# A convolutional decoder layer on 8 cores: LayerNorm steps of group A issued in pairs, with other PSUM banks

## The chip, the cores and the metric

The kernel runs on the 8 cores of one Trainium2 chip. Each core works on one prompt sequence (2064 positions: 16 meta tokens and 2048 tokens) and on 16 of the 128 sample sequences (8 positions each); the cores exchange nothing. The metric is the device time in microseconds of the slowest core. The runs of the kernel before took 1062.82, 1060.1 and 1065.99 us; the median is 1062.82.

## What is computed

One layer of a decoder with two head groups, then a convolutional FFN. The part around the change is group A:

```
h = rmsnorm(x)
a_val, a_gate, b_gate, c_gate, b_in = split(h @ w_in)
u  = a_val * sigmoid(a_gate)
ua = causal_depthwise_conv(u, width 31) + bias
ya = silu(layernorm_per_head(ua) * g + b) * beta_a        # 64 channels a head
yb = beta_b * b_gate * causal_depthwise_conv(c_gate * b_in, width 3)
x  = x + concat(ya, yb) @ w_out
h  = rmsnorm(x); up = causal_depthwise_conv(h @ w_up, width 3)
x  = x + (silu(up_gate) * up_val) @ w_down;  y = rmsnorm(x)
```

The updated convolution states are outputs as well. Weights and activations come as 32-bit floats; the large matmuls work in bf16.

## The kernel before, in words

The positions of a core are worked through in three **passes** (`PASSES`): 656 prompt positions, 768, and 640 with the 128 sample positions behind them. Channels lie on the partitions, positions on the columns. Within a pass the prompt columns are cut in two halves (`ntiles`: 328, 384 or 320 columns), and in the last pass the 128 sample columns are a third part. A pass runs through these stages: row norm and transposes; group A's input projection with the gate; group B whole; **group A's convolution and LayerNorm**; the output projection in tiles of 128 positions (`p3_tile`, L829 to L859), with the second row norm; the FFN (up projection, width-3 convolution, down projection).

All work is given to a small list (`Prog.add`): each operation names an engine, the buffers that it reads and those that it writes. Each engine executes its operations in the order of the list and waits on semaphores for the operations that it depends on. So the order of the calls is the order of every engine, and a wait holds up all that stands behind it on that engine. A PSUM bank is one buffer (`ps0` to `ps7`): a new matmul group in a bank waits until the bank's last reader is done.

Group A's stage has `nj` **jobs**: one for each of 4 channel blocks in each column part, 8 jobs in the first two passes and 12 in the last (the last four with 128 columns). Each job goes through six functions (L761 to L827):

- `s0` (L761): the width-31 convolution as 31 matmuls with diagonal weights (L773), into bank 2 or 3.
- `s0a` (L777): ScalarE adds the bias and copies to SBUF (L781, Identity).
- `s1` (L785): a matmul subtracts the mean of each head (L790), into bank 4 or 5; ScalarE squares it (L793).
- `s2` (L796): a matmul forms the variance (L800), into bank 6 or 7; ScalarE takes the square root (L804).
- `s3` (L807): VectorE takes the reciprocal (L813) and multiplies it with the centred value, which it reads from s1's bank (L815).
- `s4` (L818): ScalarE applies Silu with scale and bias (L821); VectorE multiplies by beta and writes the column block of `mixT` (L824).

The loop over `it` (L861) issues, in this order, s0 of job `it`, s3 of `it-3`, s4 of `it-4`, s2 of `it-2`, s1 of `it-1` and s0a of `it`: a software pipeline written out by hand. Sqrt and Silu need different function tables of ScalarE, so an `ACT_TABLE_LOAD` stands ahead of each change between them; Square, Identity and Copy run without one. Results of three sqrts can be held (`RB`), squares too (`t_dsq`), and two of `t_ua` and `t_yn`.

Once all convolutions are issued (`it >= nj`), each turn of the loop also issues one output tile as soon as the jobs of its columns have had s4. A tile is 4 groups of 8 matmuls (L846), each followed by VectorE's add into the residual (L850); the banks go round 0 to 3. Behind a tile stand the row norm of the tile before (`norm_stats`: ScalarE L480, L483; VectorE L485, L487) and the transposes of the tile three before (`norm_trans`, L498, L501, banks 4 and 5). In the last pass the conv states are transposed into banks 0 and 1 and stored between the loop and the remaining tiles (L874 to L892).

Of the kernel before, what the change touches and what calls it, by code (L numbers as in the profile page):

```python
# [169 lines left out]
def build(debug=False):  # L170
# [145 lines left out]
    def w_next():  # L316
        n = wcur["n"]
        wcur["n"] += 1
        assert n < wstate["issued"]
        return n, ring[n % NSLOT], f"w{n % NSLOT}"  # L320
# [170 lines left out]
    def norm_trans(j, nt, col, bsel, b):  # L491
        h = hn[bsel]
        pv = psb_bf(b).rearrange("p (k n) -> p k n", k=8)

        def f_T(e):
            ins = None
            for k in range(8):
                ins = e.transpose(out=pv[:, k, 0:nt], in_=h[0:nt, k * 128:(k + 1) * 128], identity=ident_b[0:nt, 0:nt])  # L498
            return ins
        P.add("pe", f_T, reads=[f"hn{bsel}", "ident_b"], writes=[f"ps{b}"])  # L500
        P.add("act", lambda e: e.activation(out=hT[:, :, col:col + nt], in_=pv[:, :, 0:nt], func=AF.Copy),  # L501
              reads=[f"ps{b}"], writes=[f"hT{j}"])
# [33 lines left out]
    for pi, (p0, sp, samp) in enumerate(PASSES):  # L536
# [11 lines left out]
        def ntiles_of(col, nt):  # L548
            return [t for (t, n0, nw, kind) in ntiles if n0 < col + nt and n0 + nw > col]
# [106 lines left out]
        for cp in range(2):  # L656
            for cc in range(2):
                c = cp * 2 + cc
# [98 lines left out]
        jobs = [(c, t, n0, nw, kind) for (t, n0, nw, kind) in ntiles for c in range(4)]  # L757
        RB = [(t_sig[0], "sig0"), (t_sig[1], "sig1"), (t_cg[0], "cg0")]
        nj = len(jobs)

        def s0(i):  # L761
            c, t, n0, nw, kind = jobs[i]
            b = 2 + i % 2
            rk = [f"dg{c}", f"u{c}_{t}", (f"u{c}_{t - 1}" if (kind == "p" and t > 0) else (f"uh{c}" if kind == "p" else f"ush{c}"))]

            def f_conv(e):
                ins = None
                for k in range(31):
                    if kind == "p":
                        rhs = ubuf_p[:, c, n0 + k:n0 + k + nw]  # L770
                    else:
                        rhs = ubuf_s[:, c, :, k:k + 8]
                    ins = e.matmul(ps[:, b, 0:nw], lhsT=dg[:, c * 31 + k, :], rhs=rhs, start=(k == 0), stop=(k == 30))  # L773
                return ins
            P.add("pe", f_conv, reads=rk + [LM], writes=[f"ps{b}"])

        def s0a(i):  # L777
            c, t, n0, nw, kind = jobs[i]
            b = 2 + i % 2
            sl = i % 2  # L780
            P.add("act", lambda e: e.activation(out=t_ua[sl][:, 0:nw], in_=ps[:, b, 0:nw], func=AF.Identity,  # L781
                                                bias=prm[:, PBC + c:PBC + c + 1]),
                  reads=[f"ps{b}", "prm", LM], writes=[f"ua{sl}"])

        def s1(i):  # L785
            c, t, n0, nw, kind = jobs[i]
            b = 4 + i % 2
            sl = i % 2
            s3_ = i % 3
            P.add("pe", lambda e: e.matmul(ps[:, b, 0:nw], lhsT=Cmat, rhs=t_ua[sl][:, 0:nw],  # L790
                                           start=True, stop=True),
                  reads=["Cmat", f"ua{sl}"], writes=[f"ps{b}"])
            P.add("act", lambda e: e.activation(out=t_dsq[s3_][:, 0:nw], in_=ps[:, b, 0:nw], func=AF.Square),  # L793
                  reads=[f"ps{b}", LM], writes=[f"dsq{s3_}"])

        def s2(i):  # L796
            c, t, n0, nw, kind = jobs[i]
            b = 6 + i % 2
            s3_ = i % 3
            P.add("pe", lambda e: e.matmul(ps[:, b, 0:nw], lhsT=Bd_r, rhs=t_dsq[s3_][:, 0:nw],  # L800
                                           start=True, stop=True),
                  reads=["Bd_r", f"dsq{s3_}"], writes=[f"ps{b}"])
            rb, rk_ = RB[s3_]
            P.add("act", lambda e: e.activation(out=rb[:, 0:nw], in_=ps[:, b, 0:nw], func=AF.Sqrt, bias=eps_ap),  # L804
                  reads=[f"ps{b}", "eps", LM], writes=[rk_])

        def s3(i):  # L807
            c, t, n0, nw, kind = jobs[i]
            bD = 4 + i % 2
            sl = i % 2  # L810
            s3_ = i % 3
            rb, rk_ = RB[s3_]
            P.add("dve", lambda e: e.reciprocal(out=rb[:, 0:nw], in_=rb[:, 0:nw]),  # L813
                  reads=[rk_], writes=[rk_])
            P.add("dve", lambda e: e.tensor_tensor(out=t_yn[sl][:, 0:nw], in0=ps[:, bD, 0:nw], in1=rb[:, 0:nw], op=ALU.mult),  # L815
                  reads=[f"ps{bD}", rk_, LM], writes=[f"yn{sl}"])

        def s4(i):  # L818
            c, t, n0, nw, kind = jobs[i]
            sl = i % 2  # L820
            P.add("act", lambda e: e.activation(out=t_yn[sl][:, 0:nw], in_=t_yn[sl][:, 0:nw], func=AF.Silu,  # L821
                                                scale=prm[:, PGG + c:PGG + c + 1], bias=prm[:, PGB + c:PGB + c + 1]),
                  reads=[f"yn{sl}", "prm"], writes=[f"yn{sl}"])
            P.add("dve", lambda e: e.tensor_scalar(out=mixT[:, c, n0:n0 + nw], in0=t_yn[sl][:, 0:nw],  # L824
                                                   scalar1=prm[:, PBA + c:PBA + c + 1], scalar2=None, op0=ALU.mult),
                  reads=[f"yn{sl}", "prm", LM], writes=[f"mx{c}_{t}"])

        p3 = {"idx": 0, "jo": 0, "wn4": None}
        KORD = (4, 5, 6, 7, 0, 1, 2, 3)  # L829

        def p3_tile():
            if p3["wn4"] is None:
                p3["wn4"] = [w_next() for _ in range(4)]
            wn4 = p3["wn4"]
            idx = p3["idx"]
            p3["idx"] += 1
            (j, col, nt, kind) = ttiles[idx]
            mk = [f"mx{c}_{t}" for c in range(8) for t in ntiles_of(col, nt)]
            for q in range(4):
                b = p3["jo"] % 4  # L840
                p3["jo"] += 1

                def f_mo(e, r=wn4[q][1], b=b):
                    ins = None
                    for i_, k in enumerate(KORD):
                        ins = e.matmul(ps[0:nt, b, 0:256], lhsT=mixT[:, k, col:col + nt], rhs=r[:, k, :],  # L846
                                       start=(i_ == 0), stop=(i_ == 7))
                    return ins
                P.add("pe", f_mo, reads=[wn4[q][2]] + mk + [LM], writes=[f"ps{b}"])
                P.add("dve", lambda e, b=b, q=q: e.tensor_tensor(  # L850
                    out=xres[0:nt, j, 256 * q:256 * (q + 1)], in0=ps[0:nt, b, 0:256], in1=xres[0:nt, j, 256 * q:256 * (q + 1)],
                    op=ALU.add),
                    reads=[f"ps{b}", f"xr{j}"], writes=[f"xr{j}"])
            if idx >= 3:
                (j2, col2, nt2, kind2) = ttiles[idx - 3]
                norm_trans(j2, nt2, col2, par(j2), 4 + par(j2))
            if idx >= 1:
                (j2, col2, nt2, kind2) = ttiles[idx - 1]
                norm_stats(j2, nt2, 1, par(j2))  # L859

        for it in range(nj + 4):  # L861
            for (fn, lag) in ((s0, 0), (s3, 3), (s4, 4), (s2, 2), (s1, 1), (s0a, 0)):
                if 0 <= it - lag < nj:
                    fn(it - lag)
            if it >= nj and p3["idx"] < len(ttiles):
                (j_, col_, nt_, kind_) = ttiles[p3["idx"]]
                if all(it >= 4 * t_ + 7 for t_ in ntiles_of(col_, nt_)):
                    p3_tile()
# [28 lines left out]
        while p3["idx"] < len(ttiles):  # L897
            p3_tile()
# [110 lines left out]
        jo = 0  # L1009
# [128 lines left out]
def _get_nc():  # L1138
    if "nc" not in _NC_CACHE:
        _NC_CACHE["nc"] = build()  # L1140
    return _NC_CACHE["nc"]
# [46 lines left out]
```

How the kernel before makes its waits and increments, by code:

```python
    def emit_engine(self, eng, e, semobj, final_waits=False):  # L123
        waited = {}
        for op in self.ops:
            if op.eng != eng:
                continue
            for d in op.deps:
                if waited.get(d.sem, 0) < d.val:
                    e.wait_ge(semobj[d.sem], d.val)
                    waited[d.sem] = d.val
            ins = op.fn(e)
            if op.sem is not None:
                ins.then_inc(semobj[op.sem], 16 if op.dma is not None else 1)
        if final_waits:
            for name, v in self.final_dma.items():
                k = ("dma", name)
                if waited.get(k, 0) < v:
                    e.wait_ge(semobj[k], v)
```

## Time and profile before

| | before |
|---|---|
| median of 3 runs | 1062.82 us (1060.1 to 1065.99) |
| the profiled execution | 1053.46 us |
| its span, on core 3, the slowest | 1051.9 us |
| spans of the 8 cores | 1029.4 to 1051.9 us |
| mean granted TensorE clock of the cores | 0.945 to 0.957 |
| group A's stage, passes 1, 2, 3 (first conv to first output tile) | 109.4 to 152.6, 412.7 to 461.8, 750.9 to 809.1 us |

The profile is one execution on one core, with times in us from the start of the span. A row of the groups by line names the source line, the engine, the operation, output and input, the count, the total and the mean duration, and the idle time of the engine ahead of it. The chain of waits follows the work that ended last back to its releasers and lists its pieces by time: start, duration, what. A timeline lists an engine's instructions: start, duration, engine, line, operation; in square brackets the time for which the engine had been idle and who released it. PE is TensorE, ACT ScalarE, DVE VectorE.

### The profile page before, as it was taken

The page shows a single profiled execution, that of the slowest core. Times are in us where ns is not written, and L with a number is a line of the kernel's source. Part 1 is how long each engine was busy: PE and PEld are TensorE (multiplying, and loading weights), DVE is VectorE, ACT ScalarE, POOL GpSimd, SP SyncE. Part 2 cuts the span into 40 slices and gives each one's busy share as a digit, 9 for nine tenths or more (in the row PEclk, how much of TensorE's full clock was granted, in tenths as well). Part 3 has the DMA queues.
Part 4 walks back from the last instruction along what each step waited for, and adds up shares of the span by engine and source line. Part 5 has one row for each costly group of instructions (what it writes and reads, how often), then busy time and mean ns, then how long its engine had stood idle before and what let it go on. Part 6 is the DMA issues. An engine that isn't in the chain of part 4 may idle for free.

```text
span 1051.9 us, 21154 instructions; the slowest of 8 cores (1029.4 to 1051.9 us)
## 1 busy us (share of the span) xinstructions
PE 913.3 (87%) x6993; PEld 668.0 (64%) x6993; DVE 654.4 (62%) x933; ACT 594.4 (57%) x1069; POOL 295.8 (28%) x464
## 2 busy tenths in 40 slices
PE   1769987799979899976799998979997679999997
PEld 0436655577758666555466667857766567777886
DVE  2227456499972577366399993458455548999614
ACT  3313385688871433584688872243378558888432
POOL 3003100287721213001177750023200024444200
PEclk9979988899989999988899999989997889999999
DMA  9999500889858799000878774799900067877522
GB/s 198 182 119 159 68 1 21 103 107 116 108 76 107 169 196 155 12 1 6 111 94 111 92 97 57 160 170 113 121 1 1 14 85 85 102 96 90 69 55 121
DMA packets 154569, 98.55 MB, mean 94 GB/s; under 512 B 3592, under 2 KB 148264, under 8 KB 154446
## 3 DMA queue, kind: packets, MB, share of 16 engines
q0 software_dynamic: 146688, 73.93, 56.8%
q1 hardware_dynamic: 7774, 23.27, 6.9%
q8 instruction: 58, 0.95, 0.4%
q14 instruction: 49, 0.40, 0.1%
HBM read 161.04 MB, written 10.79 MB: 163 GB/s over the span
## 4 chain that ended last, share of the span: by engine, by line
PE 67%; DMA 9%; DVE 8%; ACT 6%; issue 6%; SPq 2%; DVEq 0%; POOL 0%; ACTq 0%; POOLq 0%
PE ps L507 39%; PE ps L1018 11%; PE ps L773 9%; PE ps L846 6%; DMA arena<-sf 4%; DVE arena L955 3%; DVE arena L813 2%; SPq L349 2%; DMA yp<-arena 2%; ACT arena L480 1%; PE ps L498 1%; ACT arena L934 1%; DVE arena L487 1%; DMA ncfs<-arena 1%; DMA arena<-xs 1%
## 5 line engine op out<-in xcount | busy, mean ns | idle before, releaser
L507 PE MATMUL ps<-arena 128*128 128x328 bf16 (+3 forms) x3584 | 499.5, 302 | 18.2 <-ACT arena L620 10.6
L507 PEld LDWEIGHTS ps<-arena 128*128 128x128 bf16 x3584 | 334.9, 100 | 177.9 <-issue 25.6
L955 DVE SCALAR_TENSOR_TENSOR arena<-arena 128x656 f32<-128x656 f32 (+2 forms) x264 | 255.6, 989 | 42.0 <-ACT arena L951 19.8
L1018 PE MATMUL ps<-arena 128*128 128x256 bf16 x1496 | 166.9, 274 | 2.0 <-DVE arena L977 1.7
L1018 PEld LDWEIGHTS ps<-arena 128*128 128x128 bf16 x1496 | 146.7, 98 | 20.3 <-issue 2.7
L934 ACT ACTIVATE arena<-ps 128x328 f32<-128x328 f32 (+2 forms) x264 | 116.9, 454 | 40.4 <-PE ps L507 30.3
L303 POOL DMA_DIRECT2D arena<-w_up x66 | 57.7, 877 | 287.1 <-PE ps L846 245.6
L773 PE MATMUL ps<-arena 128*128 128x328 bf16 (+3 forms) x868 | 123.2, 301 | 0.0
L951 ACT ACTIVATE arena<-arena 128x656 f32<-128x656 f32 (+2 forms) x132 | 114.8, 902 | 7.4 <-DVE arena L925 7.4
L773 PEld LDWEIGHTS ps<-arena 128*128 128x128 bf16 x868 | 80.6, 99 | 36.7 <-issue 0.3
L813 DVE RECIPROCAL arena<-arena 128x328 f32<-128x328 f32 (+3 forms) x28 | 59.0, 2108 | 68.5 <-ACT arena L804 68.5
L846 PE MATMUL ps<-arena 128*128 128x256 bf16 (+1 forms) x576 | 79.7, 307 | 22.0 <-DVE arena L824 12.7
L846 PEld LDWEIGHTS ps<-arena 128*128 128x128 bf16 (+1 forms) x576 | 62.0, 110 | 38.1 <-issue 24.5
L1023 DVE TENSOR_TENSOR arena<-ps,arena 128x256 f32<-128x256 f32 x68 | 28.0, 423 | 89.5 <-PE ps L1018 89.3
L922 POOL COPY arena<-arena 128x2 f32<-128x2 f32 x132 | 73.1, 572 | 15.3 <-POOL arena L960 7.6
L501 ACT ACTIVATE arena<-ps 128x1024 bf16<-128x1024 bf16 (+1 forms) x36 | 35.2, 979 | 69.0 <-PE ps L498 69.0
L498 PE MATMUL ps<-arena 128*128 128x128 bf16 (+1 forms) x288 | 25.5, 243 | 52.3 <-DVE arena L487 27.0
L960 POOL COPY arena<-arena 128x2 f32<-128x2 f32 x88 | 52.1, 592 | 47.4 <-ACT arena L934 42.1
L977 DVE TENSOR_TENSOR arena<-arena 128x656 bf16<-128x656 f32 (+2 forms) x66 | 57.8, 875 | 11.1 <-ACT arena L975 6.6
L975 ACT ACTIVATE arena<-arena 128x656 f32<-128x656 f32 (+2 forms) x66 | 54.2, 822 | 18.4 <-DVE arena L955 18.1
L588 DVE TENSOR_TENSOR arena<-arena 128x1024 bf16<-128x1024 f32 (+1 forms) x48 | 56.8, 1183 | 0.0
L498 PEld LDWEIGHTS ps<-arena 128*128 128x128 bf16 (+1 forms) x288 | 20.7, 110 | 56.3 <-issue 55.6
(85 smaller groups left out, 717.5 us busy)
## 6 DMA issues: line engine op xcount, KB each, us to landing
arena<-w_up POOLq DMA_DIRECT2D x66, 512.0 KB, 8.5
arena<-w_in POOLq DMA_DIRECT2D x30, 512.0 KB, 23.3
arena<-w_down POOLq DMA_DIRECT2D x24, 512.0 KB, 7.1
arena<-xp SPq DMA_DIRECT2D x16, 512.0 KB, 10.7
yp<-arena SPq DMA_DIRECT2D x16, 512.0 KB
arena<-w_out POOLq DMA_DIRECT2D x12, 512.0 KB, 15.6
arena<-w_down POOLq DMA_DIRECT2D x12, 384.0 KB, 7.0
arena<-g SPq DMA_DIRECT2D x3, 512.0 KB, 11.7
```

The lines of the kernel that those rows point to most:

```text
L303: P.add("pool", lambda e, dst=dst, src=src: e.dma_start(out=dst, in_=src), writes=[f"w{slot}"], dma=f"ws{slot}")
L507: ins = e.matmul(ps[:, b, 0:nw], lhsT=r[:, k, off:off + 128], rhs=hT[:, k, n0:n0 + nw], start=(k == 0), stop=(k == 7))
L588: P.add("dve", lambda e: e.tensor_tensor(out=dg[:, c * 31 + k0:c * 31 + k1, :], in0=ident_f.unsqueeze(1).broadcast_to([128, nk, 128]), in1 ...
L773: ins = e.matmul(ps[:, b, 0:nw], lhsT=dg[:, c * 31 + k, :], rhs=rhs, start=(k == 0), stop=(k == 30))
L813: P.add("dve", lambda e: e.reciprocal(out=rb[:, 0:nw], in_=rb[:, 0:nw]), reads=[rk_], writes=[rk_])
L846: ins = e.matmul(ps[0:nt, b, 0:256], lhsT=mixT[:, k, col:col + nt], rhs=r[:, k, :], start=(i_ == 0), stop=(i_ == 7))
L922: P.add("pool", lambda e, rs_=rs_, ci=ci: e.tensor_copy(out=raw[rs_][:, 0:2], in_=hist_f[:, ci, :]), reads=["hist_f", LF], writes=[f"rawh{ ...
L934: P.add("act", lambda e, rs_=rs_, b=b, n0=n0, nw=nw: e.activation(out=raw[rs_][:, 2 + n0:2 + n0 + nw], in_=ps[:, b, 0:nw], func=AF.Copy), ...
L951: P.add("act", lambda e, rs_=rs_, wk=wk, fw=fw: e.activation(out=acc[rs_][:, 0:fw], in_=raw[rs_][:, 0:fw], func=AF.Copy, scale=wk[0]), rea ...
L955: P.add("dve", lambda e, rs_=rs_, wk=wk, k=k, fw=fw: e.scalar_tensor_tensor(out=acc[rs_][:, 0:fw], in0=raw[rs_][:, k:k + fw], scalar=wk[k] ...
L977: P.add("dve", lambda e: e.tensor_tensor(out=actT[:, j, 0:sp], in0=acc[rg_][:, 0:sp], in1=acc[rv_][:, 0:sp], op=ALU.mult), reads=akeys_g + ...
L1018: ins = e.matmul(ps[0:nt, b, 0:256], lhsT=actT[:, k, col:col + nt], rhs=wd3[k // 8][1][:, k % 8, :], start=(k == 0), stop=(k == 21))
```

## The change

The centred value's bank is chosen by a new function `dbank`: bank 1 for all odd jobs, banks 4 and 5 by turns for the even ones. The square root leaves `s2` and becomes a function of its own, `s2a`. s3, s4 and s2a are each issued for two jobs at once: s3 in even turns of the loop, s4 and s2a in odd turns, so that ScalarE's two Silus follow each other and its two Sqrts too. The output tiles use banks 0, 2 and 3 instead of 0 to 3.

```diff
+        def dbank(i):
+            return (4 + (i // 2) % 2) if i % 2 == 0 else 1
+
         def s1(i):
             c, t, n0, nw, kind = jobs[i]
-            b = 4 + i % 2
+            b = dbank(i)
...
             P.add("pe", lambda e: e.matmul(ps[:, b, 0:nw], lhsT=Bd_r, rhs=t_dsq[s3_][:, 0:nw],
                                            start=True, stop=True),
                   reads=["Bd_r", f"dsq{s3_}"], writes=[f"ps{b}"])
+
+        def s2a(i):
+            c, t, n0, nw, kind = jobs[i]
+            b = 6 + i % 2
+            s3_ = i % 3
             rb, rk_ = RB[s3_]
             P.add("act", lambda e: e.activation(out=rb[:, 0:nw], in_=ps[:, b, 0:nw], func=AF.Sqrt, bias=eps_ap),
                   reads=[f"ps{b}", "eps", LM], writes=[rk_])
 
         def s3(i):
             c, t, n0, nw, kind = jobs[i]
-            bD = 4 + i % 2
+            bD = dbank(i)
...
             for q in range(4):
-                b = p3["jo"] % 4
+                b = (0, 2, 3)[p3["jo"] % 3]
                 p3["jo"] += 1
...
+        assert nj % 2 == 0
         for it in range(nj + 4):
-            for (fn, lag) in ((s0, 0), (s3, 3), (s4, 4), (s2, 2), (s1, 1), (s0a, 0)):
-                if 0 <= it - lag < nj:
-                    fn(it - lag)
+            if it < nj:
+                s0(it)
+            if it % 2 == 0:
+                for i_ in (it - 4, it - 3):
+                    if 0 <= i_ < nj:
+                        s3(i_)
+            else:
+                for i_ in (it - 5, it - 4):
+                    if 0 <= i_ < nj:
+                        s4(i_)
+            if 0 <= it - 2 < nj:
+                s2(it - 2)
+            if it % 2 == 1:
+                for i_ in (it - 3, it - 2):
+                    if 0 <= i_ < nj:
+                        s2a(i_)
+            if 0 <= it - 1 < nj:
+                s1(it - 1)
+            if it < nj:
+                s0a(it)
             if it >= nj and p3["idx"] < len(ttiles):
```

## Rows read from the trace of the kernel before

**Rows 1.** The page's first part: busy us, share of the span, instructions.

```profile
PE 913.3 (87%) x6993; PEld 668.0 (64%) x6993; DVE 654.4 (62%) x933; ACT 594.4 (57%) x1069; POOL 295.8 (28%) x464
```

**Rows 2.** Groups by line, the whole span: the two table loads of the stage.

```profile
L821 ACT ACT_TABLE_LOAD x28 | 35.9, 1283 | 3.8 <-DVE arena L815 3.4
...
L804 ACT ACT_TABLE_LOAD x25 | 32.1, 1283 | 29.1 <-PE ps L800 28.8
```

**Rows 3.** Chain of waits, first pass, 105 to 200 us: start, us, what.

```profile
118.21 4.34 PE ps L773 x31
...
133.93 0.54 ACT arena L804
...
134.56 2.21 DVE arena L813
...
136.87 0.51 DVE arena L815
...
137.51 0.39 PE ps L790
137.90 4.34 PE ps L773 x31
...
152.61 5.27 PE ps L846 x32
...
171.74 5.96 PE ps L846 x32
```

**Rows 4.** Timeline of ScalarE, first pass: start, us, instruction, idle before.

```profile
134.36 0.44 ACT L793 ACTIVATE lnbuf<-ps 128x328 fp32r<-128x328 f32 x1
134.68 0.54 ACT L781 ACTIVATE lnbuf<-ps,arena 128x328 fp32r<-128x328 f32 x1
135.24 1.28 ACT L821 ACT_TABLE_LOAD   x1
136.53 0.66 ACT L821 ACTIVATE arena<-arena 128x328 f32<-128x328 f32 x1
137.28 1.28 ACT L804 ACT_TABLE_LOAD   x1
138.57 0.54 ACT L804 ACTIVATE arena<-ps,arena 128x328 f32<-128x328 f32 x1
139.00 0.44 ACT L793 ACTIVATE lnbuf<-ps 128x328 fp32r<-128x328 f32 x1
```

**Rows 5.** Timeline of VectorE, drain of the first pass.

```profile
161.09 0.38 DVE L824 TENSOR_SCALAR arena<-arena 128x328 bf16<-128x328 f32 x1
161.39 2.01 DVE L850 TENSOR_TENSOR arena<-ps,arena 128x256 f32<-128x256 f32 x4
...
164.83 2.18 DVE L813 RECIPROCAL arena<-arena 128x328 f32<-128x328 f32 x1
```

**Rows 6.** Chain of waits, whole span: last conv and two tiles, pass 2.

```profile
450.49 5.07 PE ps L773 x31
...
461.80 5.92 PE ps L846 x32
...
482.46 5.91 PE ps L846 x32
```

**Rows 7.** Chain of waits, last pass, 745 to 860 us.

```profile
797.69 3.33 PE ps L773 x31
...
809.10 6.34 PE ps L846 x32
...
823.17 3.65 PE ps L846 x32
...
831.71 4.38 DMA ncap<-arena
...
836.90 6.17 PE ps L846 x32
```

**Rows 8.** Busy time, tail of last pass: PE, PEld, DVE, ACT, POOL, clock.

```profile
788.00:809.00 21.00, 13.45 (x136) 12.34 (x137) 12.09 (x15) 20.44 (x30) 0.00 (x0) 0.81 0.00 1
```

## The prediction

> **What bounds the kernel now.** I read the page's first part, then the groups by line, then the chain of waits and the timelines of the group-A stage in each of the three passes. TensorE is busy 87% of the span and ScalarE 57% [rows 1]. ScalarE reloads its function table 25 times ahead of the Sqrt of L804 and 28 times ahead of the Silu of L821, 1.283 us each [rows 2]: 53 loads, 68.0 us of ScalarE, which the change wants to halve. What those loads cost must be read from the stage. I call the job's steps conv (L773), ident (L781), C (L790, the mean taken off), square (L793), S (L800, the variance), sqrt (L804), rec and tt (L813, L815), silu (L821), TS (L824).
>
> In the first pass the third conv starts at 118.21 and the seventh at 137.90: four jobs in 19.69 us, 9.85 for a pair [rows 3]. A conv lasts 4.34; with S and C, 0.15 each when nothing holds them, a job needs 4.64 and a pair 9.28. So TensorE loses only 0.57 us per pair here, where C waits for tt (the C at 137.51, released by the tt at 136.87 [rows 3]). One whole turn of ScalarE, from the square at 134.36 to that at 139.00 (0.43 behind the sqrt at 138.57), takes 4.64 us too, of which 2.58 are loads [rows 4]: it just keeps up. Only with the four 128-column jobs of the last pass is ScalarE the bound: busy 20.44 of 21.00 us, with a granted clock of 0.81 [rows 8]. Behind the convs comes the drain: the output projection (L846, "tiles") runs between the last jobs, and its fourth tile (p3 tile 3) waits for the last TS. It starts at 171.74 [rows 3] and 482.46 [rows 6]; VectorE is the bound there, as rec takes 2.21 us [rows 3].
>
> **The change, part by part.** *Table loads.* In the new order the pair's two silus follow each other, and the two sqrts. 28 jobs are 14 pairs: 14 loads for L804 and 14 for L821, 25 fewer, 32 us less ScalarE time, plus a few fewer in front of the Sqrt of the row norm. In the convs this is hidden (TensorE paces); on the path it could give back the 0.57 per pair and most of the last pass's tail.
>
> *The bank of the odd C.* All odd jobs' C outputs now go to bank 1, and the even ones alternate 4 and 5. C of odd job i is issued in iteration i+1; the bank's reader is tt of job i-2, which is now issued in that same iteration, second of a pair, behind two recs. Its sqrt was issued in the iteration before, behind two silus, which themselves stand behind square and ident of the iteration before that. This closes a ring from one odd C to the next. Its length at 328 columns, by starts of successive rows: C end to square 0.10, square 0.32, ident 0.55, load 1.29 [rows 4], two silus 0.55 + 0.68 (the first without a load behind it: 0.66 less the 0.11 by which neighbours overlap, as square at 134.36 and ident at 134.68), load 1.29 [rows 4]; sqrt start to rec start 0.63, rec 2.31, tt 0.43 (0.51 less an overlap), rec 2.31, tt 0.51, release 0.14, C 0.39 [rows 3]. Sum 11.50 us per pair, against 9.28 that TensorE needs and 9.85 now. The saved load is in it: without pairing only one rec stood in the ring, and C alternated between two banks.
>
> When does it bite? New conv 4 starts at 118.21 + 2 x 4.64 = 127.49 and conv 5 at 132.13. C(3) finds its bank free (tt(1) ends near 131.2, conv 4 at 131.8). Then square(3) 132.23, ident(4) 132.55, and 0.55 + 1.29 + 0.55 + 0.68 + 1.29 gives sqrt(2) at 136.91, rec at 137.54, tt(3) end at 137.54 + 5.56 = 143.10, C(5) done and conv 7 started at 143.63; before it is 142.54 (137.90 + 4.64): +1.1. C(7), one ring later, ends at 155.1 and tile 0 starts at about 155.3 against 152.61 [rows 3]: **+2.7 at the end of the convs**. For 384 columns I scale VectorE's and TensorE's durations by columns and add 0.05 to each of ScalarE's: ring 12.6 against 2 x (5.07 + 0.35) = 10.8 [rows 6]. By the same steps conv 7 starts at 451.7 instead of 450.49, and tile 0 at 464.5 instead of 461.80: +2.7. In the last pass (320 columns, then 128) four Cs are caught: conv 7 +1.1, C(7) +2.9, C(9) +5.0 (its ring still holds two 320-column recs, though the convs are short), C(11) +6.2 (its recs have 128 columns): tile 0 at 815.3 instead of 809.10 [rows 7].
>
> *The drain.* Before, VectorE alternates rec, tt, TS of one job and the four adds of a tile. Now rec and tt of the last pair stand together behind tile 1's adds and the row norm of tile 0, and both last TS behind tile 2's adds and the norm of tile 1. Pass 1: tile 0 lasts 5.27 [rows 3], S 0.35, tile 1 3.65, so tile 1's last add ends near 164.95; norm 1.5 (adds from 161.39 to next rec at 164.83, less their 2.0 [rows 5]) 166.5; rec, tt, rec, tt 5.5: 171.9. Tile 2's fourth group now shares a bank with its first (three banks 0, 2, 3 instead of four), whose add waits for this: add and release 0.6, group in the low clock and its latency 1.97, so the last add starts at 174.5; then 0.3, norm 1.5, two TS 0.75 [rows 5], release 0.15: tile 3 starts at 177.2 instead of 171.74: **+5.4**, the 2.7 above within it. Pass 2 by scaling: 487.9 instead of 482.46, +5.4. *Three banks once more:* in tile 4 the fourth group waits for the first's add, which stands behind a norm. This wait already stood at tile 5, but one more group (0.9) now lies behind it. Bounds: 0 (the add comes in time) and 2.1 (a full add chain); I take 0.9, which is one group of tile 1. Passes 1 and 2: **+6.3 each**.
>
> *Last pass.* Tile 3 needs no 128-column job. It starts near 831.3 and, its fourth group waiting for both TS and one add, ends at 835.4; before it ended at 823.17 + 3.65 = 826.8 [rows 7]: +8.6. Then the state outputs: ScalarE waits 4.38 for a DMA, and tile 4 only starts behind it at 836.90, because its first bank is bank 0, into which the transposed state goes [rows 7]. After the change its first two groups have banks 2 and 3 and can run in that wait: two groups at the low clock. Bounds 1.8 (warm groups) and 3.5 (cold, 6.17 for four of which two are quick); I take -3.0. In tile 5 the fourth group waits for an add behind a norm: +2.1. Sum **+7.7**.
>
> Total 6.3 + 6.3 + 7.7 = 20.3 us. Nothing later absorbs it: the stages behind start on the last tile's transposes, and their weights lie in the ring. The sum is made against the profiled execution, 1053.46 us with a span of 1051.9 on core 3; the median of the runs is 1062.82, 0.9% above. I add the sum to the median: **1083 us**, +1.9%. The stage's work is the same on all cores.
>
> **Clock.** In the last pass's tail short waits already bring a conv of 31 matmuls to 3.33 us and the clock to 0.81 [rows 7, 8], and tile 0 takes 5.27 and 6.34 where a warm tile takes 3.65 [rows 3, 7]: 1.2 GHz after waiting, 2.4 GHz later. The waits of the new ring (1 to 2 us each) could do this to convs 7. A conv at half speed costs 4.3 more, but S(5), sqrt(5) and rec(5) behind it come only 1 us later than rec(4) allows, so the ring hides the rest. The Trainium skill ("TensorE: Matmul & The Clock Gate", section "A second HAM failure mode: psum-queue depth-cycling") says that short idles between matmul groups, as the kernel cycles through banks, make the clock swing. The tail's 0.81 agrees, while the full convs, with waits of 0.3 us, keep their 4.34; by that rule the sum would be that of rival 4.
>
> **Rivals.**
> 1. *Faster: the loads were the limit and the bank ring isn't.* Each pair saves 2.57 us of ScalarE. If rec of the pair's first job starts so early that tt(odd) ends before the second conv, that is if the ring is below 9.3, the 0.57 per pair goes (some 2 us over the three passes), ScalarE's bound in the tail falls by half of its 8 loads (5 us), and the bank shift gives 3: about -10, **1053 us**. For it: rows 8. Against: even with C, its release, square and ident left out (1.5), 10.0 us remain in the ring: two loads, two silus, a sqrt, both recs and both tts. Chance 0.07. The Trainium skill ("ScalarE: Activation LUTs", section "Rules for kernel authors") says to group calls by table set and to do all of one before switching, and budgets about 2.7 us for a switch; by that figure 25 loads would be 67 us of ScalarE. The trace has 1.283 us a load, and the trace goes.
> 2. *The ring binds, the drain doesn't get longer* (TS and adds fill gaps I count as lost): 2.7 + 2.7 + 6.2, less 3 for the bank, is +8.6, **1071 us**. Against: VectorE's order is fixed in the program, and its idle time would sit ahead of the last pair. Chance 0.14.
> 3. *Gains and losses meet*: the ring binds by half (say 5 us in all), the tail and the bank give it back: **1063 us**. Chance 0.07.
> 4. *The clock falls in the ring and stays low through the drain*: 1 us at each conv 7, 1 to 2 us in each drain where a second tile runs slow: +5, **1088 us** or some more. Chance 0.14.
>
> **How the numbers follow.** The forecast as worked out has 0.58. The range takes in rivals 2 and 4 and the bounds of the bank terms (-3.5 to +2.1) with the runs' own spread of 3 us either side: 1069 to 1094. About 0.5% is what a measurement of this kernel can tell from no change, 1057.5 to 1068. Slower by more: 0.58 + 0.14 + 0.14 = 0.86; within: 0.07; faster: 0.07.
>
> **What would show it.** Right: loads at L804 and L821 14 each; L790 waits for L815 about 2 us at every second job from C(5) on; conv starts 4.64 apart, then pairs of 11.5; tile 3 about 5.4 us further behind the first conv; L846's idle up by some 10 us, in passes 1 and 2 partly before a fourth group; tile 4 of the last pass starting before L892 ends. Wrong: L790 not waiting for L815 in the middle of the convs, or pairs near 9.3. If sqrt starts well before the conv's end with the ring shorter, the silu spacing is my mistake; if the clock in the convs is below 0.9, rival 4.

## The result and the profile after

The changed kernel took 1085.96 us (median of 9 runs, 1078.39 to 1096.58), the kernel before 1062.09 us (10 runs) beside it. The ratio is **1.028, with a 95% interval of 1.022 to 1.034**: slower by some 23 to 36 us. The profiled execution took 1087.73 us, its slowest core (7) a span of 1086.2. The medians' difference (24 us) and the ratio (about 30 us) don't agree closely, since in some runs the cores of one die or of both have a lower granted clock and take longer, and only the ratio leaves these out (in the experiments below "four cores" are those of the undisturbed die, and four kernels have no ratio for this reason). The profiles spread less: I read three stretches in each pass, on all eight cores, and give the median over the cores.

| stretch, us (passes 1, 2, 3) | before | after | difference |
|---|---|---|---|
| first conv to tile 0 | 43.3, 49.1, 58.1 | 46.0, 51.9, 64.4 | +2.7, +2.8, +6.3 |
| tile 0 to tile 3 | 19.6, 20.6, 13.8 | 22.4, 23.1, 15.6 | +2.8, +2.5, +1.8 |
| tile 3 to the FFN's first matmul | 23.5, 24.1, 28.6 | 28.1, 29.4, 30.8 | +4.6, +5.3, +2.2 |
| sum of the nine (median of the cores' sums) | 280.9 (278.3 to 284.4) | 310.5 (306.8 to 314.0) | **+29.6** |

The sum of the nine agrees with the ratio, so the loss lies in the stage of the change. In pass 3, tiles 2 and 3 often run on without a pause, and there the start of tile 3 is interpolated, here and below. Taken from its first matmul, the changed kernel's last two stretches of pass 3 are 15.9 and 30.6 us instead of 15.6 and 30.8; the sums are not touched by this.

First the part of the page that gives the busy times, then the groups by line with the loads, C's matmul (now L793) and the tiles (now L854):

```profile
PE 928.0 (85%) x6993; PEld 676.2 (62%) x6993; DVE 655.2 (60%) x933; ACT 557.7 (51%) x1041; POOL 297.9 (27%) x464
```

```profile
L854 PE MATMUL ps<-arena 128*128 128x256 bf16 (+1 forms) x576 | 87.6, 324 | 31.4 <-DVE arena L858 25.0 <-DVE arena L832 5.7 <-ACT arena L918 0.7
...
L812 ACT ACT_TABLE_LOAD x14 | 18.0, 1283 | 0.2
L829 ACT ACT_TABLE_LOAD x14 | 18.0, 1283 | 7.1 <-DVE arena L823 6.9
...
L793 PE MATMUL ps<-lnbuf 128*128 128x328 f32 (+3 forms) x28 | 10.7, 384 | 23.5 <-DVE arena L823 23.5
...
L483 ACT ACT_TABLE_LOAD x5 | 6.4, 1283 | 0.4
```

The same two matmul groups before, C's (L790) and the tiles' (L846):

```profile
L846 PE MATMUL ps<-arena 128*128 128x256 bf16 (+1 forms) x576 | 79.7, 307 | 22.0 <-DVE arena L824 12.7 <-DVE arena L850 5.1 <-ACT arena L892 4.3
...
L790 PE MATMUL ps<-lnbuf 128*128 128x328 f32 (+3 forms) x28 | 10.9, 389 | 11.5 <-DVE arena L815 11.5
```

The loads fell as the change says: 14 and 14 instead of 53 [rows 2], and 5 instead of 8 ahead of the norm's Sqrt. ScalarE is busy 557.7 us instead of 594.4 [rows 1], and the kernel is slower: TensorE now stands idle 23.5 us ahead of C, waiting for tt (L823), instead of 11.5, and 31.4 us ahead of the tiles instead of 22.0. Of the latter, the waits for the adds (L858, before L850) rose from 5.1 to 25.0 us.

The chain of waits of pass 1 on core 7 (start, us, what) shows the first ring. The first conv starts at 112.25 here and at 109.40 before:

```profile
134.98 4.34 PE ps L773 x31
...
140.41 2.21 DVE arena L821
...
143.14 2.20 DVE arena L821
...
145.44 0.51 DVE arena L823
...
146.08 0.38 PE ps L793
146.47 4.34 PE ps L773 x31
...
151.90 2.21 DVE arena L821
...
154.62 2.20 DVE arena L821
...
156.92 0.51 DVE arena L823
...
158.18 5.67 PE ps L854 x32
```

Conv 5 starts at 134.98, right behind C(3). Conv 7 starts at 146.47, and tile 0 at 158.18: 11.49 and 11.71 us apart, with two recs ahead of each. [Rows 3] have one rec there and 9.85 us for two convs. ScalarE's timeline of the same turn:

```profile
135.07 0.44 ACT L796 ACTIVATE lnbuf<-ps 128x328 fp32r<-128x328 f32 x1 [3.49 <-PE ps L793]
135.41 0.53 ACT L781 ACTIVATE lnbuf<-ps,arena 128x328 fp32r<-128x328 f32 x1
135.96 1.28 ACT L829 ACT_TABLE_LOAD   x1
137.25 1.21 ACT L829 ACTIVATE arena<-arena 128x328 f32<-128x328 f32 x2
138.48 1.28 ACT L812 ACT_TABLE_LOAD   x1
139.78 0.96 ACT L812 ACTIVATE arena<-ps,arena 128x328 f32<-128x328 f32 x2
```

From the square at 135.07 to the first sqrt at 139.78 pass 4.71 us with one silu more than in [rows 4], and only then can the first rec start, at 140.41.

### The profile page after: what moved, and what is told of

It is laid out like the page before. It is cut to its first block, busy times and chain, and to the rows that moved or that the text cites. A ratio compares the mean times of both kernels' runs of the same rounds, so it can differ in the third digit from the quotient of the medians.

```text
span 1086.2 us, 21098 instructions; the slowest of 8 cores (1060.8 to 1086.2 us)
## 1 busy us (share of the span) xinstructions
PE 928.0 (85%) x6993; PEld 676.2 (62%) x6993; DVE 655.2 (60%) x933; ACT 557.7 (51%) x1041; POOL 297.9 (27%) x464
## 4 chain that ended last, share of the span: by engine, by line
PE 64%; DVE 12%; ACT 7%; DMA 7%; issue 7%; SPq 2%; DVEq 0%; POOL 0%; ACTq 0%; POOLq 0%
PE ps L507 35%; PE ps L1044 12%; PE ps L773 8%; PE ps L854 6%; DVE arena L981 5%; DVE arena L821 4%; DMA arena<-sf 4%; SPq L349 2%; ACT arena L480 2%; ACT arena L977 2%; PE ps L498 1%; DMA yp<-arena 1%; DMA arena<-xs 1%; DVE arena L487 1%; PE ps L793 1%
## 5 line engine op out<-in xcount | busy, mean ns | idle before, releaser
L507 PE MATMUL ps<-arena 128*128 128x328 bf16 (+3 forms) x3584 | 503.0, 304 | 17.8 <-ACT arena L620 9.8
L773 PE MATMUL ps<-arena 128*128 128x328 bf16 (+3 forms) x868 | 126.4, 307 | 0.0
L854 PE MATMUL ps<-arena 128*128 128x256 bf16 (+1 forms) x576 | 87.6, 324 | 31.4 <-DVE arena L858 25.0
L854 PEld LDWEIGHTS ps<-arena 128*128 128x128 bf16 (+1 forms) x576 | 64.8, 115 | 51.6 <-issue 35.3
L948 POOL COPY arena<-arena 128x2 f32<-128x2 f32 x132 | 75.9, 593 | 16.4 <-POOL arena L986 7.6
L986 POOL COPY arena<-arena 128x2 f32<-128x2 f32 x88 | 53.7, 610 | 47.0 <-ACT arena L960 41.1
L1001 ACT ACTIVATE arena<-arena 128x656 f32<-128x656 f32 (+2 forms) x66 | 54.3, 823 | 21.2 <-DVE arena L981 20.7
L858 DVE TENSOR_TENSOR arena<-ps,arena 128x256 f32<-128x256 f32 (+1 forms) x72 | 30.5, 423 | 46.2 <-PE ps L854 43.2
L498 PEld LDWEIGHTS ps<-arena 128*128 128x128 bf16 (+1 forms) x288 | 22.4, 116 | 56.5 <-issue 55.5
## 6 DMA issues: line engine op xcount, KB each, us to landing
arena<-w_in POOLq DMA_DIRECT2D x30, 512.0 KB, 23.5
```

Of the source, the lines that this page charges most:

```text
L507: ins = e.matmul(ps[:, b, 0:nw], lhsT=r[:, k, off:off + 128], rhs=hT[:, k, n0:n0 + nw], start=(k == 0), stop=(k == 7))
L948: P.add("pool", lambda e, rs_=rs_, ci=ci: e.tensor_copy(out=raw[rs_][:, 0:2], in_=hist_f[:, ci, :]), reads=["hist_f", LF], writes=[f"rawh{ ...
```

## The experiments

The theory after the result has three separate costs, namely the **bank ring** (all odd jobs in bank 1, behind a pair of recs), the **drain order** (the last pair stands together behind adds and norms) and a **tile ring** (three banks tie a tile's last group to an add behind a norm, and the transposes and the next norm to that group). Its rivals: the paired, late sqrts hold up the stage whatever the banks are; the lower clock; and three banks cost one group per pass, as I had predicted.

All ratios below are to the kernel before, run beside each kernel. Stretches are medians over the eight cores.

### Three banks alone: `before_three`

```diff
-                b = p3["jo"] % 4
+                b = (0, 2, 3)[p3["jo"] % 3]
```

> The kernel before, with one edit: the output tiles go round three banks (0, 2, 3) instead of four. I read three stretches in each pass: first conv to tile 0 (before 43.2, 49.2, 58.2 us), tile 0 to tile 3 (19.1, 20.7, 14.1) and tile 3 to the FFN's first matmul (23.5, 24.4, 32.2). Theory 1 (three banks close a second ring: a norm's last step, the add behind it, the tile's fourth group, the transposes, ScalarE's copy, the next norm): the last stretch grows by 4 to 5.5 us in passes 1 and 2, the middle one by about 1; pass 3 near zero, since the bank 0 wait falls away; sum 9 to 12 us, ratio 1.009 to 1.011. Theory 2 (my prediction's term: one group of 0.9 us per pass): 2 us in all, ratio 1.002. First conv to tile 0 stays within 0.3 us in both.

Measured: ratio 1.0091 [1.0056, 1.0127]. First conv to tile 0 unchanged (43.3, 49.1, 58.1), middle 19.8, 21.2, 14.8, last **28.1, 28.7, 30.7**; sum 293.6, +12.7, just above the 9 to 12 that I expected. The tile ring is right and my old term of 0.9 us is refuted. Only pass 3 went otherwise: it lost 2.1 us in the last stretch instead of nothing. The chain of waits of this kernel, tiles 4 and 5 of pass 1, shows one turn of the ring:

```profile
178.78 1.15 ACT arena L480 x2
...
180.00 1.28 ACT L483
...
182.19 1.03 issue
183.23 0.43 DVE arena L850
...
183.79 1.80 PE ps L846 x8
185.59 0.87 PE ps L498 x8
...
186.58 0.88 issue
187.46 1.15 ACT arena L480 x2
...
189.43 0.41 DVE arena L487
...
189.94 0.68 issue
190.63 0.43 DVE arena L850
...
191.19 1.03 PE ps L846 x8
```

The norm (Square L480, Sqrt L483, L487 within the issue time at 182.19), the add at 183.23, the fourth group at 183.79, the transposes behind it, ScalarE's copy of them and the next norm at 187.46, the next add at 190.63: 7.40 us for a tile whose matmuls take 3.65 [rows 7].

### Both bank changes without pairing: `banks_only`

The loop of before with `dbank` and three tile banks.

> The order of before (no pairing) with both bank changes: odd jobs' centred value in bank 1, even ones in 4 and 5 by turns, tiles on banks 0, 2, 3. Ring theory (bank 1 costs only because two reciprocals and two silus stand between two odd jobs when they are paired): first conv to tile 0 is 0.5 to 1.5 us shorter than before in each pass, not longer, and the total is that of three banks alone less 2 us. Rival (one bank for all odd jobs costs by itself): first conv to tile 0 grows by 2.7, 2.7 and about 6 us as in the changed kernel.

Measured: ratio 1.0083 [1.0055, 1.0111]; first conv to tile 0 **42.7, 48.9, 57.3**, sum 291.2. The stretch is 0.6, 0.2 and 0.8 us shorter than before, not longer (in pass 2 by less than the 0.5 that I expected at least): one bank for all odd jobs costs nothing by itself. It costs only together with the paired order.

### The changed kernel with a rotation over three banks: `after_rot3`

```diff
         def dbank(i):
-            return (4 + (i // 2) % 2) if i % 2 == 0 else 1
+            return (4, 5, 1)[i % 3]
```

> The changed kernel, with the centred value's bank chosen by i % 3 from (4, 5, 1) instead of bank 1 for all odd jobs. Then C of an odd job waits for the first tt of the pair instead of the second: one rec and one tt (2.74 us) leave the ring, which falls from 11.5 to 8.8 us, below the 9.3 of two convs. Ring theory: no wait of L793 for L823 of more than 0.5 us among the 328- and 384-column jobs, first conv to tile 0 falls from 45.9, 51.9, 64.5 to about 42.5, 48.5 and 57 us; total 10 to 14 us less than the changed kernel, ratio to before about 1.016. Rival (the late, paired sqrts hold up the stage whatever the banks): these stretches stay within 1 us of 45.9, 51.9, 64.5.

Measured: ratio 1.0107 [1.0049, 1.0166]; first conv to tile 0 **41.1, 46.9, 55.4**, sum 289.7, 20.8 below the changed kernel. The rival falls: order, sqrts and loads are those of the changed kernel, only the banks differ. The gain was larger than I wrote, since the last C (job 7) now waits for the first tt of its pair too. The first stretch also ends up 2.2, 2.2 and 2.7 us shorter than in the kernel before, so part of the 20.8 is not the bank ring of the changed kernel undone, but waits for tt that the kernel before had too. What TensorE waited for in pass 1 in this stretch and the first tile (longest first; total, times, longest), in the changed kernel (core 7) and then in this one (core 4):

```profile
PE ps L793 <- DVE arena L823: 6.5, 2, 4.5
PE ps L803 <- ACT lnbuf L796: 1.6, 1, 1.6
```

```profile
PE ps L793 <- DVE arena L823: 1.8, 1, 1.8
PE ps L803 <- ACT lnbuf L796: 1.6, 1, 1.6
```

6.5 us in two waits became 1.8 in one, ahead of tile 0; in the middle of the convs none is left.

### The changed kernel with four tile banks from tile 3 on: `after_four`

```diff
-                b = (0, 2, 3)[p3["jo"] % 3]
+                b = (p3["jo"] % 4) if idx >= 3 else (0, 2, 3)[p3["jo"] % 3]
```

> The changed kernel, with four banks (0 to 3) for the output tiles from tile 3 on (bank 1 is free by then); tiles 0 to 2 keep three. Second-ring theory: tile 3 to the FFN falls from 28.3 and 29.7 us to about 24 and 24.5 in passes 1 and 2, and the wait of the tile's fourth group for an add goes; in pass 3 tile 4 starts on bank 0 again and waits for the state outputs, so that stretch stays within 1.5 us; first conv to tile 3 unchanged; total 8 us less than the changed kernel. Rival (the last stretch is longer because of the lower clock or the two delayed TS): it stays at 28 to 30 us.

Measured: ratio 1.0206 [1.0135, 1.0276]; last stretch **23.1, 24.4, 29.6**, the first two unchanged (46.0, 22.2; 51.9, 22.9; 64.4, 15.4); sum 299.5, 11.0 below the changed kernel. The tile ring again, from the other side, in passes 1 and 2 the full 5 us each. It costs 1.2 us in pass 3, though four banks bring back the wait for the state outputs there.

### Both repairs, and more banks: `rot3_four`, `rot3_six`, `before_six`

```diff
+                b = (2, 3, 1, 0)[p3["jo"] % 4] if idx >= 3 else (0, 2, 3)[p3["jo"] % 3]
...
+                b = ((2, 3, 1, 0, 6, 7)[p3["jo"] % 6]) if idx >= 3 else ((0, 2, 3, 6, 7)[p3["jo"] % 5] if idx >= 1 else (0, 2, 3)[q % 3])
...
+                b = ((2, 3, 1, 0, 6, 7)[p3["jo"] % 6]) if idx >= 1 else q
```

(The three lines are those of the three kernels; the first two also have the rotation.)

> Both repairs in the changed kernel: centred values by i % 3 in banks 4, 5, 1, and four banks for the tiles from tile 3 on (order 2, 3, 1, 0, so that in pass 3 three groups of tile 4 come before the wait for the state outputs). If the two rings are separate costs, the stretches add up: first conv to tile 0 as with the rotation alone (41.0, 46.9, 55.2 us), tile 3 to the FFN as with four banks (23.8, 24.0, about 29), together about 280 us over the three passes against 284.4 before: ratio to before 0.995 to 1.0. If one ring only hides the other, the sum stays above 286.

> As the kernel with both repairs, but the tiles also use banks 6 and 7, free after the last sqrt (five banks from tile 1, six from tile 3). The fourth group of a tile and the first of the next no longer wait for an add behind a norm. Ring theory: tile 3 to the FFN falls below before: about 22, 22.5 and 27.5 us; sum of the stretches 275 to 278 us, ratio to before 0.99 to 0.995. Rival (with four banks ScalarE's chain of copy, square and Sqrt of each norm is what paces the last tiles): this stretch stays at 23.5 to 24.

> The kernel before with one edit: tiles from tile 1 on use six banks (2, 3, 1, 0, 6, 7). Tells whether a gain of the others comes from pairing at all. First conv to tile 0 as before (43.3, 49.1, 58.2); tile 3 to the FFN 1 to 2 us shorter per pass (tile 5's wait of 1.2 and 2.1 us for an add goes; in pass 3 three groups run in the wait for the state outputs, 1 to 3 us). Sum about 279 us, ratio 0.995. If this is as fast as the paired version, pairing brings nothing; I expect the paired one to be ahead by 5 to 8 us, from the first stretch.

Measured: `rot3_four` 0.9955 [0.9869, 1.0041], stretches 41.0, 21.8, 23.5; 46.8, 22.5, 24.4; 55.4, 15.8, 27.4, sum 277.5. The repairs add up (33.0 below the changed kernel, against 20.8 and 11.0 singly). `rot3_six` 0.9919 [0.9837, 1.0], last stretch 21.6, 22.6, 26.2, sum 274.4 (four cores). `before_six` 0.9891 [0.9814, 0.9968], 43.3, 19.6, 21.9; 49.1, 20.5, 22.2; 57.9, 14.2, 26.0, sum 274.9. Even before, the tiles were tied to their adds: six banks give 1.6, 1.9 and 2.6 us per pass. My expectation that the paired kernel would lead by 5 to 8 us failed: in the first stretch it leads by 2.2 to 2.7 us a pass, but in the middle one it gives as much back. The last experiment tells how much of this is due to the pairs.

### The last pair taken apart: `rot3_six_drain`, `after_drain`

```diff
             if it % 2 == 0:
                 for i_ in (it - 4, it - 3):
-                    if 0 <= i_ < nj:
+                    if 0 <= i_ < nj and (it, i_) != (nj + 2, nj - 2):
                         s3(i_)
...
+            if it == nj + 1:
+                s3(nj - 2)
...
-                    if 0 <= i_ < nj:
+                    if 0 <= i_ < nj and (it, i_) != (nj + 1, nj - 2):
                         s2a(i_)
...
+            if it == nj:
+                s2a(nj - 2)
```

> As before it, with the last pair taken apart: the sqrt of the last but one job is issued one turn earlier and its rec and tt ahead of tile 1's adds. My prediction said that VectorE idles ahead of the last pair and that this costs 2.7 us per pass. By that, tile 0 to tile 3 falls from about 21.8, 22.4, 15.9 us to 19 to 20, 20 to 21 and 14.5, sum of the stretches 269 to 273 us, ratio to before 0.985 to 0.99. Rival (the drain is as long because both norms and adds are VectorE work anyway): less than 0.7 us per pass.

> The changed kernel with only the last pair taken apart (sqrt of the last but one job one turn earlier, its rec and tt ahead of tile 1's adds). By the drain theory the middle stretch falls from 22.4, 23.1, 15.6 us by 1.5 to 2.7 us in passes 1 and 2, and by under 1 in pass 3; first conv to tile 0 stays at 46.0, 51.9, 64.4, since bank 1 still holds the ring; tile 3 to the FFN stays at 28.1, 29.4, 30.8. Rival (the middle stretch is long because bank 1's ring delays both last recs): it falls by less than 0.7 us.

Measured: `rot3_six_drain` 0.983 [0.968, 0.998], middle stretch 20.2, 20.6, 16.5 instead of 21.6, 22.5, 16.3, sum 270.6. `after_drain`, four cores and no ratio: 46.0, 51.9, 64.4 in the first stretch, middle **20.4, 21.6, 13.7** instead of 22.4, 23.1, 15.6. So in the changed kernel the drain's order costs 2.0, 1.5 and 1.9 us, in the full passes less than the 2.7 that I had given it, in the last more than the 1 that I expected at most; the rival's limit of 0.7 is passed. With the banks repaired the gain is less sure: pass 3 gained nothing (16.5 against 16.3), and the same kernel run once more (`best_again` below) has 20.2, 22.3 and 16.5, so that of pass 2's 1.9 us only 0.2 is left. Its single cores fall into two groups there, 20.6 and 22.3 us and above; why, the runs don't show.

### Is it the pairs or the third bank? `before_rot3_six`, `best_again`, `unpaired_again`

The order of before, centred values by `i % 3` in banks 4, 5, 1, tiles on five, then six banks.

> No pairing, but the two bank repairs: centred values by i % 3 in banks 4, 5, 1, tiles on five, then six banks. Tells whether the shorter first stretch of the paired kernels (41.1, 46.8, 55.2 us against 43.3, 49.1, 58.1) is due to the third bank or to the pairs with their halved table loads. If it is the third bank, the first stretch falls to within 0.5 us of 41.1, 46.8, 55.2 here too. If it is the pairs, it stays at 42 to 42.7, 48.5 to 49 and 57 to 58. My guess: the bank gives most of it in passes 1 and 2 (C of job 7 no longer waits for tt of job 5), and the halved loads show in pass 3, whose last jobs have 128 columns: about 41.3, 47, 57. Middle stretch 20 to 21 in passes 1 and 2; sum about 273 us.

> The same kernel as rot3_six_drain (rotation over three banks, six tile banks, last pair apart), for a narrower interval: stretches as there (41.1, 20.2, 21.2; 46.8, 20.6, 21.9; 55.2, 16.5, 26.1 us, sum 270 against 280.9 before), ratio to before 0.983 to 0.992, and below that of the unpaired kernel with six tile banks (0.9891).

> The same kernel as before_rot3_six (order of before, centred values in three banks, tiles on five, then six), for a ratio to before. Stretches as there (39.9, 21.9, 20.9; 46.1, 21.6, 21.9; 55.8, 17.2, 28.0 us), sum 271 to 274 against 280.9 before: ratio 0.990 to 0.994. If pairing were worth anything beyond the third bank, this would lie clearly above the paired version's 0.983.

Measured, four cores each: `before_rot3_six` first stretch **39.9, 46.1, 55.8**, middle 21.9, 21.7, 17.2, sum 273.0, in `unpaired_again` first stretch 39.9, 46.1, 55.8, sum 272.1; `best_again` (paired, last pair apart) 41.1, 46.8, 55.2, sum 272.6. There is no ratio for these three, so only the stretches compare them. The fairest pair for the order alone is `before_rot3_six` with 273.0 and `rot3_six` with 274.4. The unpaired kernel keeps its 53 loads:

```profile
L821 ACT ACT_TABLE_LOAD x28 | 35.9, 1283 | 3.6 <-DVE arena L815 3.1
...
L804 ACT ACT_TABLE_LOAD x25 | 32.1, 1283 | 19.4 <-PE ps L800 19.0
```

and yet its first stretch is 1.2 and 0.7 us shorter than the paired one in passes 1 and 2, and 0.6 longer in pass 3. That is all that the paired order with its halved loads is worth here. The third bank takes 3.4, 3.0 and 2.1 us off the first stretch of `before_six`, but the middle one grows by 2.3, 1.2 and 3.0 us without any pair in the order: so what the paired kernel gave back there is not the pairs' doing alone. In sum the third bank brings the unpaired order 2 to 3 us (274.9 to 273.0 and 272.1; the tiles' banks differ a little too).

## Why the prediction was right in direction and short in size

It forecast slower with 0.86 and 1083 us; 1085.96 lies in the range. That the two lie only 3 us apart is luck: the sum of its terms, 20.3 us, lies below the interval of the ratio (23 to 36) and below the 29.6 of the profiles. By the ratio, 1062.09 us become 1092, near the upper end of the range. Point by point:

1. **Bank ring: right, to a tenth.** Predicted 11.50 us a turn, measured 11.49. Conv 7 of pass 1 starts 34.22 us behind conv 0 (predicted 143.63 - 109.40 = 34.23). At tile 0 it had +2.7, +2.7, +6.2; the profiles have +2.7, +2.8, +6.3. `banks_only` and `after_rot3` show that it takes both the one bank and the paired order.
2. **Drain up to tile 3: right in sum.** Predicted +2.7, +2.7 and 1.9 (831.3 less 815.3, against 14.1), measured +2.8, +2.5, +1.8. Of that, 1.4 to 2.0 us is the order of the last pair, by `after_drain`.
3. **Three banks in the last tiles: the step that failed.** I took 0.9 us per pass, "one group of tile 1", with an upper bound of 2.1, and -0.4 for this stretch of pass 3 (7.7 less 6.2 less 1.9). Measured: +4.6, +5.3, +2.2, so 12.1 us in place of 1.4. That covers the missing 9.3 (the single stretches' medians add up to +31.0, somewhat more than the median of the sums). I followed the late fourth group to the next tile, but not to the transposes behind it on TensorE, nor to ScalarE's copy and the next norm behind those. So I took a loop for a single delay: `before_three` has it alone (+4.6, +4.6, +2.1), and `after_four` takes 5.0, 5.0 and 1.2 back.
4. **The bank 0 gain in pass 3 exists**, and the tile ring eats it. In TensorE's timeline of core 7, 16 matmuls of tile 4 run from 867.34, in the wait for the state outputs, and 16 behind it from 871.65. What is left of the tiles' wait for the outputs is 0.7 us (L918) instead of 4.3 (L892 before): 3.6 us, where I had taken 3.0.
5. **Rival 1** (loads are the limit) fell: `before_rot3_six` with all 53 loads has a sum of 273.0 us, the paired kernels with as many tile banks 270.6 to 274.4. ScalarE's time did fall, by 36.7 us, but it had cover. The Trainium skill's rule ("ScalarE: Activation LUTs", section "Rules for kernel authors") to finish one table set before switching is right about that engine's time. The 2.7 us a switch that it budgets isn't what these traces have: in ScalarE's timeline above, 1.31 us pass from the end of L781 at 135.94 to the start of L829's silu at 137.25, and 1.283 of them are the load.
6. **Rival 4** (the clock falls in the ring and stays low through the drain) is wrong for the long convs: conv 7 keeps its 4.34 us behind a wait of 1.97. In the drain the clock did fall. The busy times from tile 0 to tile 3 of pass 1, before (core 3) and after (core 7), with the granted clock right behind POOL's number:

```profile
152.61:171.74 19.13, 12.78 (x98) 9.82 (x98) 13.67 (x23) 12.90 (x18) 0.00 (x0) 0.86 0.08 27
```

```profile
158.18:180.39 22.21, 14.02 (x99) 10.35 (x99) 14.06 (x24) 10.66 (x16) 0.00 (x0) 0.73 0.08 24
```

0.86 became 0.73, in pass 2 0.83 became 0.72, and TensorE is busy 1.2 us longer in each, which is the size that the rival gave. My sum met this stretch without that term, so most of it may be hidden behind VectorE; no run separates it. In pass 3 the short convs behind waits ran slow, as before [rows 7]:

```profile
822.50 3.33 PE ps L773 x31
...
833.74 3.33 PE ps L773 x31
841.86 5.14 PE ps L854 x32
```

```profile
814.50:842.00 27.50, 17.48 (x156) 15.91 (x154) 14.71 (x17) 14.22 (x26) 0.00 (x0) 0.68 0.00 1
```

That the ring hid the clock of 0.68 there is argued from the +6.3, which was forecast without it, and not shown by a run. Rivals 2 and 3 fell with points 1 and 2.

The tile ring of point 3, as the chain of waits shows it in the changed kernel (core 7, tiles 4 and 5 of pass 1):

```profile
188.69 1.28 ACT L483
...
190.88 1.03 issue
191.91 0.43 DVE arena L858
...
192.48 1.28 PE ps L854 x8
193.75 0.87 PE ps L498 x8
...
194.75 0.88 issue
195.62 1.15 ACT arena L480 x2
...
198.79 0.43 DVE arena L858
...
199.35 1.03 PE ps L854 x8
```

From add to add, 191.91 to 198.79, are 6.88 us.

The parts are 11.8 us for the bank ring (what the first stretch lost), 12.7 for the tile ring (`before_three`; 11.0 by `after_four`) and 5.4 for the order of the last pair (`after_drain`). They add up to between 28 and 30 of the 29.6 us. So close a fit is partly luck: how the parts share the middle stretch, where they overlap, stays open.

## What to carry to other kernels

Before grouping operations to save table loads, ask whether ScalarE is on the path, and then write out the ring that each buffer closes: from the reader that frees it, through every instruction queued ahead on each engine, back to its next writer. A pair puts the second reader behind two long operations, so its buffer has to last one job longer; here a third bank shortened the first stretch by 2.1 to 3.4 us a pass, the paired order with its halved loads by 0.6 at best. Taking one bank from a rotation is no single delay when what stands behind the late group (here transposes, copy, norm) feeds the next add.

## What was not expected of the hardware

A wait of 1.97 us in the midst of long convs left the granted clock alone (the following conv took 4.34 us for 31 matmuls of 328 columns), while waits of 1.6 to 4.1 us around convs of 128 columns held its mean at 0.68 of full speed over 27.5 us. But the waits differ in length too: those of 1.60 and 4.48 us ahead of tile 0 of pass 1, with long convs before them, were followed by a granted clock of 0.63 in the next 6 us (158.00 to 164.00, core 7). Whether the length of the waits or the work around them decides is not separated by these runs.
